# One group for both directions in the levels of the recurrent stage

## The chip, the cores and the metric

The kernel runs on one core of one Trainium2 chip. The metric is the time of one execution on the device, in microseconds (us). TensorE (PE) does matmuls into PSUM, VectorE (DVE) and ScalarE (ACT) read PSUM and write SBUF, GpSimd (POOL) does elementwise work in SBUF, and SyncE (SP) issues most transfers.

## The reference

Two layers of an encoder trunk with 512 tokens and a width of 1024. Layer 0 mixes the tokens with a bidirectional recurrence (RWKV-7, 8 heads of 64) beside a gating MLP, layer 1 with differential attention; each then has cross-attention into 256 memory tokens and a gated MLP with a convolution. The change concerns the recurrence alone. For each head and each direction a 64 x 64 state is carried from token to token:

```python
def rwkv7_step(state, inp):
    r, w, k, v, kk, a = inp
    sa = jnp.einsum('...vk,...k->...v', state, -kk)
    state = (state * w[..., None, :]
             + sa[..., :, None] * (kk * a)[..., None, :]
             + v[..., :, None] * k[..., None, :])
    y = jnp.einsum('...vk,...k->...v', state, r)
    return state, y

def rwkv7_bidirectional(z, mu_prev, mu_next, w0, w2, a0, a2, g2, k_k, k_a, r_k, out_gain):
    ...
    state0 = jnp.zeros((2, bsz, H, N, N), jnp.float32)
    _, ys = lax.scan(rwkv7_step, state0, xs)
    y = ys[:, 0] + jnp.flip(ys[:, 1], axis=0)
    y = rms_norm(jnp.transpose(y, (1, 0, 2, 3)), out_gain).astype(z.dtype)
    bonus = jnp.sum(rh[:, :, None] * kh * r_k, axis=(2, 4))
    out = (y + bonus[..., None] * vh).reshape(bsz, seq, RWKV_WIDTH)
    return out * g
```

## The kernel before

All is fp32. The large products of the rest of the kernel run as three fp32r products (`gemm_pe`, line 369), with the weights split by ScalarE and VectorE. Between them lies the recurrent stage, `pair_pe`, `pair_act`, `pair_dve` and `pair_pool`, once for each of NJ = 4 pairs of heads.

The recurrence isn't run token by token. The 512 tokens are cut in chunks of CH = 64. In a chunk the dependence of each token on the earlier ones is a triangular 64 x 64 matrix, and the kernel needs the inverse of (I - A). For a pair of heads there are 2 directions (d = 0 forward, 1 backward) x 8 units (head and token tile) x 2 halves of the partitions (x), 32 blocks of 64 x 64. A tile such as UU has the shape [128, 2, 8, 64]: one direction is 128 x 512, both are 128 x 1024.

The inverse is built by doubling. `gram_dve` (line 1170) makes AI, and the first U and T, which are right inside blocks of 2. Then LV = 5 levels double the block size. A level does:
- X: TensorE multiplies AI by U for each block (line 938), direction 0 into PSUM bank 0 and direction 1 into bank 2;
- mask: VectorE multiplies that by the level's 0/1 mask into XX (line 1231), one instruction for each direction, when `p_x` tells that the direction's 16 matmuls are done;
- U: TensorE multiplies T by XX (line 952) into the same bank, when `p_xm` tells that the direction's mask is done;
- T: TensorE multiplies the other way round (line 958) into banks 1 and 3, except at the last level;
- copies: ScalarE copies U (line 1071) and T (line 1075) of each direction back to SBUF, which releases the next level's X (`p_u0`, `p_u1`) and U (`p_t0`, `p_t1`) for that direction.

The order on TensorE is written out: X of direction 0, X of direction 1, `side_pe` (work of this or the next pair that fits in between), `chain_pe` (a step of the chunk-to-chunk chain of the previous pair), then U and T of direction 0, U and T of direction 1, `side_pe` and `chain_pe` again. In pair 0 there is no chain, in pair 3 there is no next pair to prepare, so there the gaps hold less. Side work and chain use banks 4 to 7. After the levels the product at line 972 multiplies U by AXT, waiting for each direction's U, and a tail of small products (lines 980 and 1010) and the next pair's Gram products (lines 832 and 844) follow. VectorE does in a level the two masks, then the additions of the chain (lines 877 and 881), and from level 2 on the next pair's decay scan, keys and scaling (`prep_scan_dve`, `prep_key_dve`, `prep_scale_dve`). ScalarE does in a level side copies, the copies of U and T, side copies. Each fp32 product shows as two MATMUL rows in the trace, so a group of 16 is x32 there.

Of the kernel before, what the change touches and what calls it, by code (L numbers as in the profile page):

```python
# [25 lines left out]
P = 128  # L26
# [64 lines left out]
def build(nc, a, out):  # L91
# [718 lines left out]

    def mask24(name):
        return rk(name).unsqueeze(1).unsqueeze(1).to_broadcast([P, 2, NT, CH])
# [113 lines left out]
    def pair_pe(T, j):  # L926
        e = T.e
        gram_pe(T, j)
        for lv in range(LV):
            for d in range(2):  # L930
                e.wait_ge(S(f"p_u{d}"), j * (LV + 1) + lv + 1)
                if lv == 0 and d == 0:
                    e.wait_ge(S("p_bfree"), 2 * j + 2)
                if lv == 0 and d == 1 and j > 0:
                    e.wait_ge(S("p_qfree"), j)
                for u in range(8):
                    for x in range(2):
                        mm = e.matmul(PS[xs(x), 2 * d, u * CH:u * CH + CH], AI[xs(x), d, u, :], UU[xs(x), d, u, :],  # L938
                                      start=True, stop=True)
                mm.then_inc(S("p_x"), 1)  # L940
            side_pe(T, j, 2 * lv)
            if j > 0 and 1 <= 2 * lv <= STEPS:
                chain_pe(e, j - 1, 2 * lv)
            for d in range(2):
                e.wait_ge(S("p_xm"), 2 * (j * LV + lv) + d + 1)
                if lv == 0:
                    e.wait_ge(S("p_tt"), 2 * j + d + 1)
                else:
                    e.wait_ge(S(f"p_t{d}"), j * (LV - 1) + lv)
                for u in range(8):  # L950
                    for x in range(2):
                        mm = e.matmul(PS[xs(x), 2 * d, u * CH:u * CH + CH], TT[xs(x), d, u, :], XX[xs(x), d, u, :],  # L952
                                      start=True, stop=True)
                mm.then_inc(S(f"p_un{d}"), 1)
                if lv < LV - 1:
                    for u in range(8):
                        for x in range(2):
                            mm = e.matmul(PS[xs(x), 2 * d + 1, u * CH:u * CH + CH], XX[xs(x), d, u, :], TT[xs(x), d, u, :],  # L958
                                          start=True, stop=True)
                    mm.then_inc(S(f"p_tn{d}"), 1)  # L960
# [6 lines left out]
        for d in range(2):  # L967
            e.wait_ge(S(f"p_u{d}"), (j + 1) * (LV + 1))
# [96 lines left out]
    def pair_act(A, j):  # L1065
        e = A.e
        for lv in range(LV):
            side_act(A, j, 2 * lv)
            for d in range(2):
                e.wait_ge(S(f"p_un{d}"), j * LV + lv + 1)  # L1070
                e.activation(UU[:, d, :, :], PS[:, 2 * d, :].rearrange("p (u k) -> p u k", k=CH), ACT.Copy)\
                    .then_inc(S(f"p_u{d}"), 1)
                if lv < LV - 1:
                    e.wait_ge(S(f"p_tn{d}"), j * (LV - 1) + lv + 1)
                    e.activation(TT[:, d, :, :], PS[:, 2 * d + 1, :].rearrange("p (u k) -> p u k", k=CH), ACT.Copy)\
                        .then_inc(S(f"p_t{d}"), 1)
            side_act(A, j, 2 * lv + 1)
# [92 lines left out]
    def gram_dve(V, j):  # L1170
# [10 lines left out]
        for d in range(2):  # L1181
            V.mine(e.tensor_tensor(AI[:, d, :, :], AI[:, d, :, :], mask8("ident2"), ALU.add))
            V.wait_mine()
            e.tensor_tensor(UU[:, d, :, :], UU[:, d, :, :], mask8("ident2"), ALU.add).then_inc(S(f"p_u{d}"), 1)
# [40 lines left out]
    def pair_dve(V, j):  # L1225
        e = V.e
        gram_dve(V, j)
        for lv in range(LV):
            for d in range(2):
                e.wait_ge(S("p_x"), 2 * (j * LV + lv) + d + 1)  # L1230
                e.tensor_tensor(XX[:, d, :, :], PS[:, 2 * d, :].rearrange("p (u k) -> p u k", k=CH),
                                mask8(f"X{'fb'[d]}{lv + 2}"), ALU.mult).then_inc(S("p_xm"), 1)
# [832 lines left out]
```

## Time and profile before

| what | value |
|---|---|
| median of 3 runs | 1934.67 us (1932.86 to 1935.8) |
| the profiled execution | 1930.15 us, span 1928.3 us |
| mean granted TensorE clock | 0.981 of full |
| busy: TensorE | 1807.2 us (94%) |
| busy: VectorE, ScalarE, GpSimd | 997.2, 778.8, 100.9 us |
| chain that ended last | TensorE 86%, VectorE 7%, ScalarE 3%, issue 2% |
| of it line 369 / 952 / 958 / 938 | 67% / 2% / 2% / 1% |
| recurrent stage | 177 to 421 us |

Busy time is the time in which an engine's rows cover the clock; the end of a matmul row is modelled. The chain is followed back from the last instruction to what released each step. A row of the timeline gives start, length, engine, line, operation, tiles, how many instructions it merges, and in brackets how long the engine was idle ahead of it and what ended that.

### The profile page before, as it was taken

The numbers are of one execution on the slowest core, as the hardware profiler recorded it, in microseconds if no ns is written. First come the engines' busy times: TensorE is split into PE (matmuls) and PEld (weight loads), VectorE is DVE, ScalarE is ACT, GpSimd is POOL, SyncE is SP. The second block draws the span as 40 slices with busy tenths as digits, with TensorE's granted clock in tenths as the row PEclk, the third lists the DMA queues.
The fourth block names the chain that finished last, engine by engine and source line by source line (L and its number), as shares of the span: only waits on it lengthen the run. The fifth ranks groups of instructions, "written<-read, shape, count | busy, mean of one in ns | idle before, by whom it ended". The sixth has DMA issues, their size and how long they took to land.

```text
span 1928.3 us, 32260 instructions
## 1 busy us (share of the span) xinstructions
PE 1807.2 (94%) x14281; PEld 1494.3 (77%) x14281; DVE 997.2 (52%) x1355; ACT 778.8 (40%) x1166; POOL 100.9 (5%) x79
## 2 busy tenths in 40 slices
PE   4998998889899999999998999999999999999999
PEld 4877887777777878888887887567777878888887
DVE  4477555547524355634553444795524346543662
ACT  3243443343554244422432333774545244422441
POOL 1001111100000000000000022000000000000000
PEclk9999999989999999999999999999999999999999
DMA  6310000033322223322322222002322122233222
GB/s 209 98 44 1 4 3 4 4 112 119 110 88 88 66 66 110 109 88 88 90 97 98 88 88 88 1 1 75 123 87 88 54 77 88 91 109 107 87 77 76
DMA packets 96453, 149.41 MB, mean 77 GB/s; under 512 B 3479, under 2 KB 50170, under 8 KB 96314
## 3 DMA queue, kind: packets, MB, share of 16 engines
q1 hardware_dynamic: 95018, 142.41, 22.5%
q0 software_dynamic: 1296, 4.95, 0.8%
q8 instruction: 112, 1.84, 0.4%
q14 instruction: 27, 0.22, 0.0%
HBM read 145.25 MB, written 2.10 MB: 76 GB/s over the span
## 4 chain that ended last, share of the span: by engine, by line
PE 86%; DVE 7%; ACT 3%; issue 2%; DMA 1%; POOL 0%; ACTq 0%; DVEq 0%; POOLq 0%; SPq 0%
PE PS L369 67%; PE PS L1452 3%; PE PS L952 2%; PE PS L958 2%; PE PS L1469 1%; PE PS L938 1%; PE PS L1338 1%; PE PS L1312 1%; PE PS L495 1%; DMA WRAW<-ab_w_in 1%; PE PS L980 1%; PE PS L972 1%; DVE LOS L444 1%; PE PS L1459 1%; DVE WLO L338 1%
## 5 line engine op out<-in xcount | busy, mean ns | idle before, releaser
L338 DVE TENSOR_TENSOR WLO<-WRAW,WHI 128x2048 fp32r<-128x2048 f32 (+1 forms) x132 | 296.5, 2250 | 445.2 <-ACT WHI L330 445.2
L330 ACT ACTIVATE WHI<-WRAW 128x2048 fp32r<-128x2048 f32 (+1 forms) x132 | 248.0, 1881 | 484.5 <-PE PS L369 451.2
L369 PE MATMUL PS<-HIS,WHI 128*128 128x512 f32 x856 | 333.8, 390 | 1.5 <-DVE SM L1699 1.5
L369 PE MATMUL PS<-HIS,WLO 128*128 128x512 f32 x856 | 333.0, 389 | 0.0
L369 PE MATMUL PS<-LOS,WHI 128*128 128x512 f32 x856 | 333.0, 389 | 0.0
L369 PE MATMUL PS<-WHI,HIS 128*128 128x512 f32 x608 | 238.9, 393 | 11.0 <-DVE LOS L444 4.0
L369 PE MATMUL PS<-WHI,LOS 128*128 128x512 f32 x608 | 238.0, 391 | 0.0
L369 PE MATMUL PS<-WLO,HIS 128*128 128x512 f32 x608 | 237.9, 391 | 0.0
L369 PEld LDWEIGHTS PS<-HIS,WHI 128*128 128x128 f32 x856 | 160.7, 188 | 35.2 <-DVE SM L1699 1.9
L369 PEld LDWEIGHTS PS<-HIS,WLO 128*128 128x128 f32 x856 | 160.7, 188 | 33.6
L369 PEld LDWEIGHTS PS<-LOS,WHI 128*128 128x128 f32 x856 | 160.7, 188 | 33.4 <-issue 0.2
L369 PEld LDWEIGHTS PS<-WHI,HIS 128*128 128x128 f32 x608 | 114.9, 189 | 37.6 <-DVE LOS L444 4.4
L369 PE MATMUL PS<-WHI,GHI 128*128 128x512 f32 x352 | 136.9, 389 | 0.0
L369 PE MATMUL PS<-WHI,GLO 128*128 128x512 f32 x352 | 136.9, 389 | 0.0
L369 PE MATMUL PS<-WLO,GHI 128*128 128x512 f32 x352 | 136.9, 389 | 0.0
L369 PEld LDWEIGHTS PS<-WLO,HIS 128*128 128x128 f32 x608 | 115.0, 189 | 24.2
L369 PEld LDWEIGHTS PS<-WHI,LOS 128*128 128x128 f32 x608 | 114.9, 189 | 23.6
L502 DVE TENSOR_TENSOR X<-X,PS 128x512 f32<-128x512 f32 x64 | 42.9, 684 | 70.6 <-PE PS L369 70.6
L369 PEld LDWEIGHTS PS<-WLO,GHI 128*128 128x128 f32 x352 | 66.1, 188 | 13.8
L369 PEld LDWEIGHTS PS<-WHI,GLO 128*128 128x128 f32 x352 | 66.1, 188 | 13.7
L369 PEld LDWEIGHTS PS<-WHI,GHI 128*128 128x128 f32 x352 | 66.1, 188 | 13.7
L1415 ACT ACTIVATE GHI<-SG 128x512 fp32r<-128x512 f32 x44 | 27.8, 633 | 108.9 <-DVE SG L1435 108.9
(281 smaller groups left out, 2519.0 us busy)
## 6 DMA issues: line engine op xcount, KB each, us to landing
WRAW<-ffn_w_up SPq DMA_DIRECT2D x88, 512.0 KB, 4.7
WRAW<-ffn_w_down SPq DMA_DIRECT2D x20, 1024.0 KB, 5.0
WRAW<-cross_wkv SPq DMA_DIRECT2D x16, 1024.0 KB, 5.0
WRAW<-diff_w_in SPq DMA_DIRECT2D x12, 1024.0 KB, 5.1
WRAW<-ab_w_in SPq DMA_DIRECT2D x10, 1024.0 KB, 5.3
WRAW<-cross_wq SPq DMA_DIRECT2D x8, 1024.0 KB, 5.0
WRAW<-cross_wo SPq DMA_DIRECT2D x8, 1024.0 KB, 5.1
X<-x SPq DMA_DIRECT2D x8, 512.0 KB, 9.1
```

The source lines that it names most:

```text
L330: A.e.activation(part(WHI[i % 3], i), part(WRAW[i % 2], i), ACT.Copy).then_inc(S("w_hi"), 1)
L338: V.e.tensor_tensor(part(WLO[i % 3], i), part(WRAW[i % 2], i), part(WHI[i % 3], i).bitcast(F32), ALU.subtract).then_inc(S("w_lo"), 1)
L369: mm = e.matmul(o, l, r, start=(si == 0 and kk == 0 and q == 0), stop=(si == len(steps) - 1 and kk == nk - 1 and q == 2))
L444: e.scalar_tensor_tensor(lo(k)[:, 0:nt * P], PS[:, b0 + k % 4, 0:nt * P], gain(k), hi(k)[:, 0:nt * P].bitcast(F32), ALU.mult, ALU.subtract ...
L495: mm = e.transpose(PS[:, b0 + k % 4, t * P:t * P + P], xn[:, t, k * P:k * P + P], ident)
L502: V.e.tensor_tensor(o, o, PS[:, bank_base(name, gi) + b, :], ALU.add).then_inc(sem(name, "ev"), 1)
L938: mm = e.matmul(PS[xs(x), 2 * d, u * CH:u * CH + CH], AI[xs(x), d, u, :], UU[xs(x), d, u, :], start=True, stop=True)
L952: mm = e.matmul(PS[xs(x), 2 * d, u * CH:u * CH + CH], TT[xs(x), d, u, :], XX[xs(x), d, u, :], start=True, stop=True)
L958: mm = e.matmul(PS[xs(x), 2 * d + 1, u * CH:u * CH + CH], XX[xs(x), d, u, :], TT[xs(x), d, u, :], start=True, stop=True)
L972: mm = e.matmul(PS[xs(x), 2 * d + u // 4, (u % 4) * P:(u % 4) * P + P], UU[xs(x), d, u, :], AXT[xs(x), d, u, :], start=True, stop=True)
L1415: A.e.activation(GHI[2 * gi + b - 2][:, :], SG[b - 2][:, :], ACT.Copy).then_inc(sem(name, "hi"), 1)
L1452: e.matmul(PS[:, b + c, :], QF[:, h, c, t * P:t * P + P], KF[:, h, :], start=True, stop=True).then_inc(S("dl"), 1)
```

## The change

The two directions are no longer two groups. At each level TensorE does the X of both directions (banks 0 and 1) and signals once; VectorE multiplies both by their masks in one instruction of 1024 columns (`mask2x8` addresses the forward and backward mask with one stride); TensorE then does U of both directions, signals, T of both directions (banks 2 and 3), signals; ScalarE copies U of both in one instruction and T of both in another. The first U of a pair (`gram_dve`) is signalled once, after both directions (`p_u0`). The product at line 972 waits for the one copy of U. The matmuls are the same in number and shape.

```diff
--- before.py
+++ after.py
@@ -807,6 +807,12 @@
 
     def mask8(name):
         return rk(name).unsqueeze(1).to_broadcast([P, 8, CH])
+
+    def mask2x8(lv):
+
+        o = RK[f"Xf{lv}"][0]
+        by = RK["Xb2"][0] - RK["Xf2"][0]
+        return RC[:, o:o + 2 * by].rearrange("p (d k) -> p d k", d=2)[:, :, 0:CH].unsqueeze(2).to_broadcast([P, 2, 8, CH])
 
     def mask24(name):
         return rk(name).unsqueeze(1).unsqueeze(1).to_broadcast([P, 2, NT, CH])
@@ -927,37 +933,40 @@
         e = T.e
         gram_pe(T, j)
         for lv in range(LV):
+            if lv == 0:
+                e.wait_ge(S("p_u0"), j + 1)
+                e.wait_ge(S("p_bfree"), 2 * j + 2)
+                if j > 0:
+                    e.wait_ge(S("p_qfree"), j)
+            else:
+                e.wait_ge(S("p_un"), j * LV + lv)
             for d in range(2):
-                e.wait_ge(S(f"p_u{d}"), j * (LV + 1) + lv + 1)
-                if lv == 0 and d == 0:
-                    e.wait_ge(S("p_bfree"), 2 * j + 2)
-                if lv == 0 and d == 1 and j > 0:
-                    e.wait_ge(S("p_qfree"), j)
                 for u in range(8):
                     for x in range(2):
-                        mm = e.matmul(PS[xs(x), 2 * d, u * CH:u * CH + CH], AI[xs(x), d, u, :], UU[xs(x), d, u, :],
+                        mm = e.matmul(PS[xs(x), d, u * CH:u * CH + CH], AI[xs(x), d, u, :], UU[xs(x), d, u, :],
                                       start=True, stop=True)
-                mm.then_inc(S("p_x"), 1)
+            mm.then_inc(S("p_x"), 1)
             side_pe(T, j, 2 * lv)
             if j > 0 and 1 <= 2 * lv <= STEPS:
                 chain_pe(e, j - 1, 2 * lv)
+            e.wait_ge(S("p_xm"), j * LV + lv + 1)
+            if lv == 0:
+                e.wait_ge(S("p_tt"), 2 * j + 2)
+            else:
+                e.wait_ge(S("p_tn"), j * (LV - 1) + lv)
             for d in range(2):
-                e.wait_ge(S("p_xm"), 2 * (j * LV + lv) + d + 1)
-                if lv == 0:
-                    e.wait_ge(S("p_tt"), 2 * j + d + 1)
-                else:
-                    e.wait_ge(S(f"p_t{d}"), j * (LV - 1) + lv)
                 for u in range(8):
                     for x in range(2):
-                        mm = e.matmul(PS[xs(x), 2 * d, u * CH:u * CH + CH], TT[xs(x), d, u, :], XX[xs(x), d, u, :],
+                        mm = e.matmul(PS[xs(x), d, u * CH:u * CH + CH], TT[xs(x), d, u, :], XX[xs(x), d, u, :],
                                       start=True, stop=True)
-                mm.then_inc(S(f"p_un{d}"), 1)
-                if lv < LV - 1:
+            mm.then_inc(S("p_u"), 1)
+            if lv < LV - 1:
+                for d in range(2):
                     for u in range(8):
                         for x in range(2):
-                            mm = e.matmul(PS[xs(x), 2 * d + 1, u * CH:u * CH + CH], XX[xs(x), d, u, :], TT[xs(x), d, u, :],
+                            mm = e.matmul(PS[xs(x), 2 + d, u * CH:u * CH + CH], XX[xs(x), d, u, :], TT[xs(x), d, u, :],
                                           start=True, stop=True)
-                    mm.then_inc(S(f"p_tn{d}"), 1)
+                mm.then_inc(S("p_t"), 1)
             side_pe(T, j, 2 * lv + 1)
             if j > 0 and 2 * lv + 1 <= STEPS:
                 if lv == 0:
@@ -965,7 +974,7 @@
                 chain_pe(e, j - 1, 2 * lv + 1)
 
         for d in range(2):
-            e.wait_ge(S(f"p_u{d}"), (j + 1) * (LV + 1))
+            e.wait_ge(S("p_un"), (j + 1) * LV)
             e.wait_ge(S("p_ax"), 2 * j + d + 1)
             for u in range(8):
                 for x in range(2):
@@ -1066,14 +1075,13 @@
         e = A.e
         for lv in range(LV):
             side_act(A, j, 2 * lv)
-            for d in range(2):
-                e.wait_ge(S(f"p_un{d}"), j * LV + lv + 1)
-                e.activation(UU[:, d, :, :], PS[:, 2 * d, :].rearrange("p (u k) -> p u k", k=CH), ACT.Copy)\
-                    .then_inc(S(f"p_u{d}"), 1)
-                if lv < LV - 1:
-                    e.wait_ge(S(f"p_tn{d}"), j * (LV - 1) + lv + 1)
-                    e.activation(TT[:, d, :, :], PS[:, 2 * d + 1, :].rearrange("p (u k) -> p u k", k=CH), ACT.Copy)\
-                        .then_inc(S(f"p_t{d}"), 1)
+            e.wait_ge(S("p_u"), j * LV + lv + 1)
+            e.activation(UU[:, :, :, :], PS[:, 0:2, :].rearrange("p d (u k) -> p d u k", k=CH), ACT.Copy)\
+                .then_inc(S("p_un"), 1)
+            if lv < LV - 1:
+                e.wait_ge(S("p_t"), j * (LV - 1) + lv + 1)
+                e.activation(TT[:, :, :, :], PS[:, 2:4, :].rearrange("p d (u k) -> p d u k", k=CH), ACT.Copy)\
+                    .then_inc(S("p_tn"), 1)
             side_act(A, j, 2 * lv + 1)
         for d in range(2):
             e.wait_ge(S("p_wu"), 2 * j + d + 1)
@@ -1181,7 +1189,8 @@
         for d in range(2):
             V.mine(e.tensor_tensor(AI[:, d, :, :], AI[:, d, :, :], mask8("ident2"), ALU.add))
             V.wait_mine()
-            e.tensor_tensor(UU[:, d, :, :], UU[:, d, :, :], mask8("ident2"), ALU.add).then_inc(S(f"p_u{d}"), 1)
+            i = e.tensor_tensor(UU[:, d, :, :], UU[:, d, :, :], mask8("ident2"), ALU.add)
+        i.then_inc(S("p_u0"), 1)
         for d in range(2):
             e.tensor_tensor(TT[:, d, :, :], AI[:, d, :, :], mask8(M_T1[d]), ALU.mult).then_inc(S("p_tt"), 1)
 
@@ -1226,10 +1235,9 @@
         e = V.e
         gram_dve(V, j)
         for lv in range(LV):
-            for d in range(2):
-                e.wait_ge(S("p_x"), 2 * (j * LV + lv) + d + 1)
-                e.tensor_tensor(XX[:, d, :, :], PS[:, 2 * d, :].rearrange("p (u k) -> p u k", k=CH),
-                                mask8(f"X{'fb'[d]}{lv + 2}"), ALU.mult).then_inc(S("p_xm"), 1)
+            e.wait_ge(S("p_x"), j * LV + lv + 1)
+            e.tensor_tensor(XX[:, :, :, :], PS[:, 0:2, :].rearrange("p d (u k) -> p d u k", k=CH), mask2x8(lv + 2),
+                            ALU.mult).then_inc(S("p_xm"), 1)
             if lv == 0:
                 gram_k_dve(V, j)
             for s in (2 * lv, 2 * lv + 1):
```

On TensorE, in level 1 of pair 0, the row that begins an X group (lines 938 and 946) waits for U, the row that begins a U group (952 and 960) for T and for the mask; L817 and L823 are the side work. Before:

```order
L938 MATMUL PS<-UU,AI 64x64 [waits p_u0]
L938 MATMUL PS<-UU,AI 64x64 x15
L938 MATMUL PS<-UU,AI 64x64 [waits p_u1]
L938 MATMUL PS<-UU,AI 64x64 x15
L817 MATMUL PS<-ZS_86,WL_71 128x512 [waits p_bonfree]
L817 MATMUL PS<-ZS_86,WL_71 128x512
L952 MATMUL PS<-XX,TT 64x64 [waits p_t0,p_xm]
L952 MATMUL PS<-XX,TT 64x64 x15
L958 MATMUL PS<-TT,XX 64x64 x16
L952 MATMUL PS<-XX,TT 64x64 [waits p_t1,p_xm]
L952 MATMUL PS<-XX,TT 64x64 x15
L958 MATMUL PS<-TT,XX 64x64 x16
```

And with the change, in the same place on TensorE:

```order
L946 MATMUL PS<-UU,AI 64x64 [waits p_un]
L946 MATMUL PS<-UU,AI 64x64 x31
L823 MATMUL PS<-ZS_86,WL_71 128x512 [waits p_bonfree]
L823 MATMUL PS<-ZS_86,WL_71 128x512
L960 MATMUL PS<-XX,TT 64x64 [waits p_tn,p_xm]
L960 MATMUL PS<-XX,TT 64x64 x31
L967 MATMUL PS<-TT,XX 64x64 x32
```

The T product of direction 0 moved from ahead of the U product of direction 1 to behind it, and a level has two rows that wait for another engine's work on X or U where it had four.

On ScalarE, from the copies of level 3 of pair 0 to those of WU after level 4 (TMP is the exponentials of the next pair, AXT side work), before:

```order
L1071 ACTIVATE UU<-PS 128x512 [waits p_un0]
L1075 ACTIVATE TT<-PS 128x512 [waits p_tn0]
L1071 ACTIVATE UU<-PS 128x512 [waits p_un1]
L1075 ACTIVATE TT<-PS 128x512 [waits p_tn1]
L1033 ACT_TABLE_LOAD
L1033 ACTIVATE TMP_109<-TMP_111 128x1024 [waits p_c]
L1035 ACTIVATE TMP_111<-TMP_111 128x1024 [waits p_e]
L1062 ACTIVATE AXT<-PS 128x8x64 [waits p_x0] x2
L1071 ACTIVATE UU<-PS 128x512 [waits p_un0]
L1071 ACTIVATE UU<-PS 128x512 [waits p_un1]
L1080 ACTIVATE WU_97<-PS 128x1024 [waits p_wu]
```

The same stretch of ScalarE with the change:

```order
L1079 ACTIVATE UU<-PS 128x1024 [waits p_u]
L1083 ACTIVATE TT<-PS 128x1024 [waits p_t]
L1042 ACT_TABLE_LOAD
L1042 ACTIVATE TMP_109<-TMP_111 128x1024 [waits p_c]
L1044 ACTIVATE TMP_111<-TMP_111 128x1024 [waits p_e]
L1071 ACTIVATE AXT<-PS 128x8x64 [waits p_x0] x2
L1079 ACTIVATE UU<-PS 128x1024 [waits p_u]
L1088 ACTIVATE WU_97<-PS 128x1024 [waits p_wu]
```

Nothing changed places here; four copies became two, and the two after level 4 became one, which waits for the U product of both directions.

## Rows read from the trace of the kernel before

**Rows 1.** Waits of TensorE, 177 to 421 us: waited for, total us, times, longest.
```profile
PE PS L952 <- DVE XX L1231: 7.9, 8, 2.0
PE PS L1010 <- issue: 6.5, 4, 1.9
...
PE PS L938 <- DVE UU L1184: 4.8, 8, 1.3
PE PS L980 <- issue: 4.8, 4, 1.3
```

**Rows 2.** Windows: stretch, its us, busy us of each engine, clock, DMA.
```profile
178.00:181.00 3.00, 3.00 (x76) 3.00 (x72) 1.82 (x3) 0.00 (x0) 0.00 (x0) 0.50 0.02 5
238.00:241.00 3.00, 2.13 (x76) 1.89 (x68) 2.97 (x6) 0.00 (x0) 0.00 (x0) 1.00 0.00 0
177.00:421.00 244.00, 214.65 (x6934) 196.82 (x6931) 126.96 (x211) 92.72 (x147) 30.23 (x21) 0.99 0.03 7
```

**Rows 3.** Timeline of level 2, pair 0: start, us, engine, line, work.
```profile
201.50 2.08 PE L938 MATMUL PS<-UU,AI 64*64 64x64 f32 x64
...
203.63 0.69 DVE L1231 TENSOR_TENSOR XX<-PS,RC 128x512 f32<-128x512 f32 x1 [0.24 <-PE PS L938]
...
204.15 1.15 PE L952 MATMUL PS<-XX,TT 64*64 64x64 f32 x32
...
209.06 2.08 PE L938 MATMUL PS<-UU,AI 64*64 64x64 f32 x64
```

**Rows 4.** Single lines: length in ns, least, median, most.
```profile
L1071 ACT ACTIVATE UU<-PS x40: 597/597/601, 189.0 to 404.7; 128x512 f32<-128x512 f32 x40
...
L1141 DVE TENSOR_TENSOR KAP<-TMP,TMP x4: 1210/1210/1215, 158.8 to 348.7; 128x1024 f32<-128x1024 f32 x4
...
L1080 ACT ACTIVATE WU<-PS x8: 1024/1026/1030, 223.7 to 408.2; 128x1024 f32<-128x1024 f32 x8
```

**Rows 5.** Timeline of level 0, pair 0, TensorE.
```profile
185.90 1.15 PE L938 MATMUL PS<-UU,AI 64*64 64x64 f32 x32 [0.18 <-DVE UU L1184]
...
187.70 1.15 PE L952 MATMUL PS<-XX,TT 64*64 64x64 f32 x32 [0.66 <-DVE XX L1231]
```

**Rows 6.** Timeline: U of level 3 pair 0, level 2 pair 1, level 1 pair 3.
```profile
212.09 1.15 PE L952 MATMUL PS<-XX,TT 64*64 64x64 f32 x32
...
259.81 2.03 PE L938 MATMUL PS<-UU,AI 64*64 64x64 f32 x64
...
261.89 0.69 DVE L1231 TENSOR_TENSOR XX<-PS,RC 128x512 f32<-128x512 f32 x1 [0.24 <-PE PS L938]
...
262.93 1.10 PE L952 MATMUL PS<-XX,TT 64*64 64x64 f32 x32
...
376.37 1.80 PE L938 MATMUL PS<-UU,AI 64*64 64x64 f32 x56
...
378.70 1.10 PE L952 MATMUL PS<-XX,TT 64*64 64x64 f32 x32
```

**Rows 7.** Timeline of level 3, pair 1 (pair 2 reads alike).
```profile
273.23 1.26 DVE L1231 TENSOR_TENSOR XX<-PS,RC 128x512 f32<-128x512 f32 x2
273.95 1.15 PE L952 MATMUL PS<-XX,TT 64*64 64x64 f32 x32 [1.98 <-DVE XX L1231]
```

**Rows 8.** Timeline of level 4: pair 0, pair 1 and pair 3.
```profile
219.55 1.95 PEld L952 LDWEIGHTS PS<-XX,TT 64*64 64x64 f32 x64
...
221.66 3.59 PE L972 MATMUL PS<-AXT,UU 64*64 64x128 f32 x61
...
282.51 2.08 PE L952 MATMUL PS<-XX,TT 64*64 64x64 f32 x64 [0.64 <-DVE XX L1231]
...
284.42 3.55 PE L972 MATMUL PS<-AXT,UU 64*64 64x128 f32 x61
...
402.60 2.03 PE L952 MATMUL PS<-XX,TT 64*64 64x64 f32 x64
...
404.47 3.55 PE L972 MATMUL PS<-AXT,UU 64*64 64x128 f32 x62
```

## The prediction

> **What bounds the kernel now.** I read the waits of TensorE first, then the stage as a whole, then single levels in order of time. The change touches only the recurrent stage, from 177 to 421 us of a span of 1928.3 us. There TensorE has work for 214.65 of 244 us, VectorE for 126.96, ScalarE for 92.72, and the granted clock is 0.99, the 2.4 GHz level [rows 2]. The reader should see that TensorE's idle time in this stage is short and has few causes: 7.9 us until a mask of VectorE (8 times), 4.8 us until the first U of a pair is ready (8 times), and some 14 us in which nothing held it but its own instructions, 6.5 us of it at line 1010 and 4.8 us at line 980 [rows 1]. No row there shows TensorE waiting for a copy of U or T, except for a few tenths after the last level.
>
> Now a single level, level 2 of pair 0 [rows 3]. TensorE starts the X group of both directions at 201.50. VectorE starts the mask of the second direction at 203.63, 2.13 us after the group began. But the mask of the first direction has been ready for long, and TensorE goes from X through its side work straight into the first U group at 204.15, 2.65 us after X began, and into the next X at 209.06, with no wait on those rows. So in such a level **TensorE's issue is the bound**, and the split in two directions is what hides the mask: the first direction's mask runs under the second direction's matmuls. The same split hides the copies.
>
> **The change, part by part.** No matmul is removed. A level loses one mask instruction and two copies (one at level 4), and gets wide ones.
>
> *Wide instructions.* A mask of 512 columns releases U 0.72 us after its start (273.23 to 273.95) [rows 7]. For 1024 columns the nearest row is VectorE's product at line 1141, 1.21 us; with the same 0.03 us of hand-over that gives 1.24 us. The copy of 512 columns takes 0.60 us and the 1024-column copy of line 1080 takes 1.03, so 0.43 more [rows 4]. These have the same source and type, so I take them as they are; the upper bound is twice a narrow one (0.69 and 0.60, so 1.38 and 1.20, 0.17 more each) [rows 3, 4], and no row supports less than 1.21 and 1.03, which are the lower ends too.
>
> *The mask before U.* The wide mask can start only when the X of both directions is done: 2.13 us after X began in pair 0 [rows 3], 2.08 us in the later pairs, where no idle or switch stands ahead (259.81 to 261.89) [rows 6]. So U can't start before X + 3.37 us in pair 0 and X + 3.32 us in the others. What covers this is TensorE's side and chain work between X and U. Where it is shorter, the difference is new idle time.
> - Level 0: there is no side work, and the first X also waits now for the U of both directions, so it starts at 185.90 instead of 184.57. 185.90 + 2.13 + 1.24 = 189.27 against 187.70 [rows 5]: 1.57 us, alike in all four pairs, **6.28 us**.
> - Level 1: in pair 0 the distance from X to U is 3.07 us (it lacks a chain step), so 0.30. In pairs 1 and 2 it is over 3.5, so nothing. In pair 3 there is no next pair to prepare, and it is 378.70 - 376.37 = 2.33 [rows 6], so 0.99. **1.29 us**.
> - Level 2: pair 0 has 2.65 us [rows 3], so 0.72. The others have 262.93 - 259.81 = 3.12 [rows 6], so 0.20 each. **1.32 us**.
> - Level 3: pair 0 has 212.09 - 209.06 = 3.03 [rows 3, 6], so 0.34. In pairs 1 and 2 VectorE is late with its scans and the mask starts at 273.23 in any case [rows 7]; U follows 1.24 instead of 0.72 later, 0.52 each. Pair 3 has 3.5, nothing. **1.38 us**.
> - Level 4: side work (line 922, as many rows as X) makes the distance from X to U four groups too, 3.73, in pairs 0 and 3, nothing there. In pairs 1 and 2 VectorE's keys are late as at level 3 and U waited already (0.64 us on its row) [rows 8]: 0.52 each, counted in the next item.
>
> *The copy after U.* At levels 0 to 3 the copy of U has the whole T group and the side work of TensorE to hide in: it is ready 2.13 + 1.03 + 0.12 = 3.28 us after U began, the next X starts 3.73 us after it at the earliest (four groups of 0.93, from 2.08 for 64 rows less 1.15 for 32 [rows 5, 8]). The copy of T has the next X and its mask. Both cost nothing; if that cover were gone, 0.43 us plus half a group each. After level 4 there is no T, and line 972 waits for U. Today the first direction's copy is enough to start it. Now U of both must be done (0.93 us more, a group of 64 rows takes 2.08 and one of 32 takes 1.15) [rows 5, 8] and be copied (0.43 more): 1.36 us in pair 3 (404.47 to 405.83). With the late mask, 0.52 + 1.36 = 1.88 in pairs 1 and 2 each. In pair 0 ScalarE is late with its exponentials, which hides a part: U is done at 219.55 + 2.08 = 221.63, its copy releases line 972 at 222.78 against 221.66 [rows 8], 1.12. **6.24 us**.
>
> *VectorE's and ScalarE's other work.* Behind each mask on VectorE stand the K masks (level 0), the chain's additions and the next pair's preparation; they start up to 0.6 us later against X, but later X groups are later too, and TensorE waits for them only where it is counted above. On ScalarE line 1041, 1027 and 1048 follow the copies with over 0.3 us to spare. SP and POOL get no instruction moved; the first load of the next weights waits for the end of this stage and moves with it.
>
> Sum: 6.28 + 1.29 + 1.32 + 1.38 + 6.24 = **16.5 us slower**. The profiled execution, 1930.15 us, would become 1946.7. The median of the runs shown is 4.5 us above that execution, so for the median I say 1934.67 + 16.5 = 1951.2 us.
>
> A rule that speaks for the change: two masks in a row cost 1.26 us on VectorE [rows 7], because the second overlaps the first, against 1.21 for a wide one [rows 4], so 0.05 us is saved per level. The Trainium skill (VectorE: DVE Perf Modes, "The TRN2 errata") says that each instruction pays a fixed latency once, so that one large tile is cheaper than two small ones; by its formula for fp32, an estimate, a merge saves 0.157 us, 3.1 us over 20 levels. The trace shows a third of it, on an engine that is idle for half of the stage.
>
> **The rivals.**
> 1. *Faster: the ring of three engines is the bound, not TensorE's issue.* If X, mask, U, copy and the next X were one chain at every level, then merging saves the fixed costs: 0.05 us for each of 20 masks and 2 x 0.60 - 1.03 = 0.17 for each of 36 copies, 7.1 us, giving 1927.6. It decides from the point where the *second* direction's mask or copy ends after TensorE's own work. Against it: between 201.50 and 209.06 TensorE has none of these waits [rows 3], and 7.9 us in all stand on masks [rows 1].
> 2. *TensorE's code comes too late in the tail of each pair, and takes up the new waits.* Lines 980 and 1010 hold four gaps each, in the middle of groups that wait for no semaphore [rows 1]. If they are code that is not loaded yet, a wait just ahead of them lets it arrive. The new wait before line 972 could then hide the first gap of each pair: 4.8 us back, 1946.4. If all 11.3 us went, 1939.9. Against it: the stretch before line 972 is slower than the tail, so its code is there in time already, and the matmuls are as many as before. The Trainium skill (Runtime: NRT & Kernel Launch, "Instruction fetch mechanics") says that code fetch is hidden, as an engine dispatches slower than the code comes in. By that there would be no such gaps, nothing would be given back, and the sum would stand; the 6.5 and 4.8 us speak against the page.
> 3. *The clock falls in the new gaps.* At 1.2 GHz (granted 0.50) 76 rows of line 844 and its neighbours filled 3.00 us, at the full clock 76 rows filled 2.13 [rows 2]. If each pair ran some 9 us around level 4 at the low clock, that is 4 x 3 x 0.87 = 10.4 us more, 1961.6. Against it: from 238 to 241 TensorE was idle for almost a third and kept 1.00 [rows 2], and the longest new gap is under 3 us.
> 4. *No difference*, within 4 us: everything that adds is hidden by the late code and the chain of VectorE. It needs rival 2 in full (5.2 us are left) and 1.3 us more, 1938.6 or less.
>
> **How the numbers follow.** The forecast has 0.73, rival 1 has 0.05, rival 2 has 0.11, rival 3 has 0.06 and rival 4 has 0.05. The bounds of the wide instructions are 0.17 for the mask in the 15 levels that count (2.6 us) and 4 x 0.17 for copies (0.7); a session's median moves by 2 us, as the runs and the profiled execution show. That gives 1946.5 to 1956 for the forecast alone; rival 2's first case lies at its lower edge, and the range is 1945 to 1957. A measurement of this kernel can tell about 0.2% (3.9 us) from no change. Slower 0.90, within it 0.06, faster 0.04 (rival 1, less what its saving is too small to show).
>
> **What would show it.** Waits of the U group for the mask rise from 7.9 to some 15 us, with 1.3 us at level 0 of each pair and 2.5 at level 3 of pairs 1 and 2. The waits of the first X of a pair rise from 4.8 to some 9 us. The group of line 972 gets a wait for ScalarE's U of 1.1 us in each pair, 4.6 us in all, where there was none. The mask takes 1.21 us and starts 2.1 us after X; U and T copies take 1.03. TensorE's busy time in the stage stays at 215 us and the stage grows by 16.5. I am wrong if the gaps at lines 980 and 1010 shrink by several us (rival 2), if matmul rows get longer (rival 3), or if the wide mask takes well over 1.4 us.

## The result, and the profile after

The changed kernel takes 1949.43 us (median of 4 runs, 1946.98 to 1952.37); the kernel before, beside it, 1933.76 us (4 runs, 1930.38 to 1935.8). The ratio is 1.0088, 95% interval 1.0069 to 1.0107: slower by about 17.0 us (the medians differ by 15.7). The prediction was 16.5 us slower, 1951.2 us in a range of 1945 to 1957. The profiled execution takes 1946.98 us, against 1930.15 for that of before.

The page of the changed kernel, its span and the busy time of the engines:

```profile
span 1945.2 us, 32181 instructions
...
PE 1807.0 (93%) x14281; PEld 1494.5 (77%) x14281; DVE 994.8 (51%) x1335; ACT 772.2 (40%) x1130; POOL 99.9 (5%) x79
```

The span grew by 16.9 us. The waits of TensorE in the recurrent stage of the changed kernel, 177 to 441 us (line waited for, total us, times, longest), answer to [rows 1]; lines 946, 960, 989 and 1019 are the 938, 952, 980 and 1010 of before:

```profile
PE PS L960 <- DVE XX L1239: 14.8, 12, 2.5
PE PS L946 <- DVE UU L1192: 10.0, 4, 2.6
PE PS L1019 <- issue: 6.5, 4, 1.9
PE PS L989 <- issue: 5.3, 4, 1.6
PE PS L981 <- ACT UU L1079: 4.5, 4, 1.1
```

Three rows changed, and they are the three that the working named: the mask 7.9 to 14.8 us, the first X of a pair 4.8 to 10.0, and a new wait of 4.5 us for the copy of U. The two rows of gaps in which TensorE waits for no other engine stayed: 6.5 and 6.5, 4.8 and 5.3. The three are 14.8 + 10.0 + 4.5 = 29.3 us now and were 7.9 + 4.8 = 12.7: 16.6 us more, against the 16.9 us by which the span grew.

The stage as a whole, from the first Gram row of pair 0 to the first row of the chain behind the last tail, before and changed (us, busy us of PE, PEld, DVE, ACT and POOL, clock, DMA):

```profile
176.72:418.18 241.46, 212.52 (x6880) 195.15 (x6881) 125.35 (x205) 92.72 (x147) 30.23 (x21) 0.99 0.02 4
```

```profile
175.40:436.00 260.60, 214.59 (x6880) 196.54 (x6881) 122.95 (x185) 86.63 (x111) 29.31 (x21) 0.98 0.02 4
```

Between these two marks the stage is 19.1 us longer. TensorE does the same 6880 matmul rows in 214.59 us, 2.1 more than before; its idle time grew from 28.9 to 46.0 us, by 17.1. VectorE and ScalarE have 2.4 and 6.1 us less to do. So nearly all of the added time is idle time of TensorE.

Level 2 of pair 0, the stretch of [rows 3], in the timeline of the changed kernel:

```profile
201.89 2.08 PE L946 MATMUL PS<-UU,AI 64*64 64x64 f32 x64
...
204.01 1.22 DVE L1239 TENSOR_TENSOR XX<-PS,RC 128x1024 f32<-128x1024 f32 x1 [7.12 <-PE PS L946]
...
205.29 2.08 PE L960 MATMUL PS<-XX,TT 64*64 64x64 f32 x64 [0.68 <-DVE XX L1239]
...
207.42 1.02 ACT L1079 ACTIVATE UU<-PS 128x1024 f32<-128x1024 f32 x1 [1.68 <-PE PS L960]
```

The wide mask starts 2.12 us after X and lasts 1.22; U starts 3.40 us after X, where it was 2.65. Before the change the first mask ran under the second direction's matmuls; now nothing of X is left to run under it. The copy of U ends at 208.44 and the next X comes at 210.20, so that copy is hidden, as forecast.

Level 0 of pair 0 [rows 5] in the changed kernel, with both new waits one behind the other:

```profile
184.34 2.08 PE L946 MATMUL PS<-UU,AI 64*64 64x64 f32 x64 [2.60 <-DVE UU L1192]
...
186.47 1.23 DVE L1239 TENSOR_TENSOR XX<-PS,RC 128x1024 f32<-128x1024 f32 x1 [0.98 <-PE PS L946]
...
187.75 2.08 PE L960 MATMUL PS<-XX,TT 64*64 64x64 f32 x64 [1.33 <-DVE XX L1239]
```

The wide instructions themselves (ns: least, median, most), against [rows 4]:

```profile
L1239 DVE TENSOR_TENSOR XX<-PS,RC x20: 1197/1224/1225, 186.5 to 417.2; 128x1024 f32<-128x1024 f32 x20
```

```profile
L1079 ACT ACTIVATE UU<-PS x20: 1023/1023/1027, 190.0 to 420.9; 128x1024 f32<-128x1024 f32 x20
```

They took 1.224 and 1.023 us; 1.21 and 1.03 were borrowed from other lines.

Level 3 of pair 1 [rows 7] and level 4 of pair 1 [rows 8] in the changed kernel:

```profile
279.21 2.08 PE L960 MATMUL PS<-XX,TT 64*64 64x64 f32 x64 [2.51 <-DVE XX L1239]
```

```profile
288.30 2.08 PE L960 MATMUL PS<-XX,TT 64*64 64x64 f32 x64 [1.18 <-DVE XX L1239]
291.50 3.60 PE L981 MATMUL PS<-AXT,UU 64*64 64x128 f32 x61 [1.12 <-ACT UU L1079]
```

Waits of 1.98 and 0.64 us became 2.51 and 1.18, 0.53 and 0.54 more. The product after the levels starts 3.20 us after U instead of 1.91.

### The profile page after: what moved, and what is told of

The parts are those of the page before. It is cut to its first block, busy times and chain, and to the rows that moved or that the text cites. A ratio compares the mean times of both kernels' runs of the same rounds, so it can differ in the third digit from the quotient of the medians.

```text
span 1945.2 us, 32181 instructions
## 1 busy us (share of the span) xinstructions
PE 1807.0 (93%) x14281; PEld 1494.5 (77%) x14281; DVE 994.8 (51%) x1335; ACT 772.2 (40%) x1130; POOL 99.9 (5%) x79
## 3 DMA queue, kind: packets, MB, share of 16 engines
q0 software_dynamic: 1296, 4.95, 0.8%
## 4 chain that ended last, share of the span: by engine, by line
PE 84%; DVE 8%; ACT 4%; issue 2%; DMA 2%; POOL 0%; ACTq 0%; POOLq 0%; SPq 0%; DVEq 0%
PE PS L369 64%; PE PS L1460 3%; PE PS L960 2%; PE PS L946 2%; PE PS L967 2%; PE PS L1477 1%; PE PS L1346 1%; DVE WLO L338 1%; PE PS L495 1%; PE PS L1320 1%; DVE XX L1239 1%; DMA WRAW<-ab_w_in 1%; PE PS L989 1%; PE PS L981 1%; DMA WRAW<-cross_wq 1%
```

## The experiments

The sizes below are distances between starts of groups on TensorE, read from the timelines: X to U, U to the product after the levels, Gram to the first X of a pair. Ratios are to the kernel before, measured beside each kernel on the same chip. Each kernel has one profile (the changed kernel two), and its execution is not always near the median of the timed runs.

### One part undone at a time

**x_mask**: the changed kernel with one mask per direction, each signalled and waited for alone (VectorE's side is shown; U of a direction waits for its own mask).

```diff
+            for d in range(2):
+                e.wait_ge(S("p_x"), 2 * (j * LV + lv) + d + 1)
+                e.tensor_tensor(XX[:, d, :, :], PS[:, d, :]..., mask8(f"X{'fb'[d]}{lv + 2}"), ALU.mult)...
```

> The changed kernel with the X group and the mask by direction again: TensorE signals X of each direction, VectorE masks 512 columns at a time, U of a direction waits for its own mask. Copies and the first U stay wide. Theory A (TensorE goes without a gap as long as something covers the mask; what costs is that nothing of U can start before X of both directions is done and masked): U follows X after 1.9 us instead of 3.4 at level 0, and at the other levels as soon as the side work ends, which gives back 4 x 1.5 at level 0, and 1.4, 1.5, 1.4 and 1.1 us at levels 1 to 4, 11.5 us: about 1938. Theory B (the cost is in the order U, U, T, T, the banks, or the wide copies): under half of it comes back, over 1943.

Measured: 1939.2 us, ratio 1.0042 (1.003 to 1.0055). TensorE's waits in the stage:

```profile
PE PS L946 <- DVE UU L1192: 9.9, 4, 2.6
...
PE PS L960 <- DVE XX L1240: 5.3, 4, 2.0
```

The wait for the mask is gone except at levels 3 and 4 of pairs 1 and 2, and the distance from X to U at levels 1 to 4 is that of before to 0.01 us (3.07, 2.66, 3.04, 3.73 in pair 0). The first X still waits 9.9 us. 8.9 us came back (1.0088 less 1.0042), where 11.5 were expected. At level 0 the expected 1.9 us came in pairs 0 and 1 (1.94 each); in pairs 2 and 3 X to U was 2.70 and 3.41, and the granted clock had fallen to 0.50 there (at 309.6 and 374.4 us) and once at level 3 of pair 1 (at 275.4). So the wide mask carries about half of the loss. The parts are not quite separate: 1.94 is also 1.19 below the 3.13 of the kernel before, since both first U are ready when X begins.

**x_copy**: after level 4 alone, U of each direction is signalled and copied by itself, with direction 1 in bank 2 there (levels 0 to 3 stay wide).

> The changed kernel with U of the last level copied by direction, each copy with its own signal, and with direction 1 in bank 2 at that level. Theory A: the first product after the levels starts 1.9 us after U instead of 3.2 (1.1 in pair 0), 5.0 us in all: about 1944.5. Theory B (the first half of that product would wait for something else, such as AXT): no difference, 1949.

Measured: 1949.4 us, ratio 1.0089 (1.0074 to 1.0103), no gain. Yet the edit did what it was for: U to the product after the levels is 2.47, 1.91, 1.92 and 1.87 us in the four pairs, where the changed kernel has 3.16 to 3.20: 4.5 us. The gain went somewhere else, and TensorE's timeline of level 0, pair 0, shows where:

```profile
184.60 2.55 PE L946 MATMUL PS<-UU,AI 64*64 64x64 f32 x64 [2.63 <-DVE UU L1201]
...
188.47 2.83 PE L960 MATMUL PS<-XX,TT 64*64 64x64 f32 x48 [1.32 <-DVE XX L1248]
```

The same waits as in the changed kernel, but the matmuls are slower: 64 rows of X take 2.55 instead of 2.08. X to U is 3.87, 4.91, 4.56 and 4.57 us in the four pairs, where the changed kernel has 3.41 each time. With the next U to X, the slow rows at level 0 cost 7.5 us. This is the clock; it has a part of its own below. The profile explains the loss inside the stage (261.98 us long, the changed kernel 260.60). This execution, 1943.52 us, is also the fastest of the six: outside the stage it took 1679.7 us, the changed kernel 1684.6. Why the median lies 5.9 us higher stays open.

**x_first**: the first U of a pair is signalled by direction again.

> The changed kernel with the first U of a pair signalled by direction. X of direction 0 starts 1.3 us earlier in each pair, but the wide mask waits for X of direction 1, which ends 0.9 to 1.0 us earlier. Theory A: 4 x 0.95 = 3.8 us back, about 1945.6. Theory B (VectorE's own order holds the mask back, which stands behind the T masks): under 1 us, 1949.

Measured: 1944.7 us, ratio 1.0067 (1.0053 to 1.008). The wait of the first X falls from 10.0 to 4.9 us; X to U of level 0 grows from 3.41 to 3.71, since the second direction's X now starts with its own late U.

**x_all3**: these three undone together. What stays of the change: one wide copy of U at levels 0 to 3 and one of T, the other banks, and the order U, U, T, T on TensorE.

> The three together: masks, first U and last copy by direction. What stays of the change is its banks, its order U, U, T, T, and one wide copy of U (levels 0 to 3) and of T. Theory A says that those are hidden and cost nothing: the time of the kernel before, 1933.8 within 2 us. Theory B: 1938 or more.

Measured: 1930.05 us, ratio 0.9995 (0.9986 to 1.0005), 12 runs. TensorE's waits:

```profile
PE PS L961 <- DVE XX L1249: 7.9, 8, 2.0
...
PE PS L947 <- DVE UU L1202: 4.5, 4, 1.4
```

The rows are those of before (7.9 and 4.8). The whole loss is in the three merged hand-overs; the copies at levels 0 to 3, the banks and the order of the matmuls together cost at most 1.0 us and give at most 2.7. Rival 1, a ring of engines as the bound, would have the wide copies gain 0.17 us each, 5.4 us for 32: the interval excludes it.

### What is left where VectorE is late

**early_before** and **early_after**: the next pair's preparation on VectorE goes between the two chain steps of its level, in the kernel before and in the changed one.

```diff
             for s in (2 * lv, 2 * lv + 1):
                 if j > 0 and 1 <= s <= STEPS:
                     chain_dve(e, j - 1, s)
-            if j + 1 < NJ and lv >= 2:
-                (prep_scan_dve, prep_key_dve, prep_scale_dve)[lv - 2](V, j + 1)
+                if j + 1 < NJ and lv >= 2 and s == 2 * lv:
+                    (prep_scan_dve, prep_key_dve, prep_scale_dve)[lv - 2](V, j + 1)
```

> The kernel before with one line moved on VectorE: in levels 2 to 4 the next pair's scan, keys and scaling stand between the two additions of the chain instead of behind both. Nothing else differs. Theory A (at levels 3 and 4 of pairs 1 and 2 the mask is late only since that work is queued behind an addition that waits for TensorE, while VectorE idles): the distance from X to U falls from 5.65 to 3.5 us at level 3 and from 4.55 to 3.7 at level 4, 5.9 us in all: about 1928. Theory C (VectorE has too much work there in any order, or GpSimd slows it): under 2 us, 1932 or more.

> The same move in the changed kernel. Theory A: from 6.18 to 3.5 us at level 3 and from 5.08 to 3.7 at level 4 of pairs 1 and 2, 8.0 us in all: about 1941.5, so that the part of the change that was paid there (2.1 us) is not paid any more and the distance to the kernel before with the same move is 13.5 to 14.5 us. Theory C: under 2 us.

Measured: early_before 1923.98 us, ratio 0.9964 (0.995 to 0.9978): faster than both kernels. X to U at level 3 of pairs 1 and 2 falls from 5.65 to 3.50 us, at level 4 from 4.55 to 3.73, 2 x (2.15 + 0.82) = 5.9 us in all. The timeline of early_before:

```profile
263.76 0.69 DVE L1102 TENSOR_SCALAR TMP<-TMP 128x1024 f32<-128x1024 f32 x1
...
268.71 2.03 PE L938 MATMUL PS<-UU,AI 64*64 64x64 f32 x64
...
269.85 0.69 DVE L1231 TENSOR_TENSOR XX<-PS,RC 128x512 f32<-128x512 f32 x1 [0.64 <-PE PS L938]
```

And of the kernel before, the same instruction and its neighbour on GpSimd:

```profile
268.03 2.36 POOL L1152 TENSOR_TENSOR BET<-KK,TMP 128x1024 f32<-128x1024 f32 x1 [6.14 <-PE PS L914]
...
268.72 2.22 DVE L1102 TENSOR_SCALAR TMP<-TMP 128x1024 f32<-128x1024 f32 x1
```

The instruction took 2.22 us, now 0.69, and it no longer stands ahead of the mask: it now comes 4.7 us before GpSimd's product, in a stretch in which VectorE was idle. In the kernel before it ended at 270.94, 0.55 us after GpSimd's product (270.39). The Trainium skill (SBUF — State Buffer, "Who interferes with whom") says that this kind of VectorE instruction can take the port pair shared with GpSimd, and that the one of the two that comes second blocks fully until the first is done. The trace agrees in time: 1.67 of the 2.22 us lie under GpSimd's product, and all four of these instructions take 0.68 to 0.69 us in early_before. How much of the gain comes from this and how much from the new place was not tested apart.

early_after: 1944.35 us, ratio 1.0066 (1.0053 to 1.0078): about 4.3 us back (1.0088 less 1.0066) where 8.0 were expected, and about 20 us above early_before where 13.5 to 14.5 were expected. The same distances came down (3.50 and 3.73), but X to U at level 0 of pairs 2 and 3 is 4.57 and 4.25 instead of 3.41, with the clock down at 311.6 and 376.5 us; with a slower U to X in pair 3 that is 3.6 us.

**cover_after**: the changed kernel with the VTK half of line 980's products, which needs no U, put ahead of the product that waits for the copy.

> The changed kernel with the products of GKR and VTK, which need no U, moved from behind the first product after the levels to ahead of it. They fill TensorE's wait for the wide copy. Theory A (the wide copy of U costs only because nothing covers it): 4 x 1.0 = 4.0 us back, about 1945.4. Theory B (the copy delays the tail in another way, or the code of the tail comes later then): no difference.

Measured: 1950.87 us, ratio 1.01 (1.0085 to 1.0114), no gain. The cover is there (TensorE goes from U straight into it):

```profile
225.21 2.03 PE L960 MATMUL PS<-XX,TT 64*64 64x64 f32 x64
227.20 1.16 PE L980 MATMUL PS<-GKR,VTK 64*64 64x64 f32 x64
228.37 3.60 PE L1001 MATMUL PS<-AXT,UU 64*64 64x128 f32 x62
```

The stretch from that product to the next Gram is 1.8, 1.5 and 1.4 us shorter in the first three pairs. But level 0 is slow in all four pairs: X to U 3.90, 4.03, 4.95 and 4.51, with the next U to X 8.8 us lost in all.

### The clock at level 0

Two experiments that removed a stall of TensorE without touching level 0, x_copy and cover_after, had lost their gain at level 0, and early_after a part of it. To see whether the changed kernel does this by itself, it ran unedited once more.

> The changed kernel once more, beside the next three. Theory K (in the merged kernels TensorE idles twice around the first X of a pair, and in some executions the clock falls to the 1.2 GHz level there, as in the traces of x_copy and cover_after, at a different number of pairs each time): 1.0088 of the kernel before, with one or more pairs whose distance from the first X to U is over 3.5 us. Theory A alone: the same time, and 3.41 us in every pair.

Measured: 1951.88 us, ratio 1.0091 (1.0076 to 1.0106). Windows of level 0, pair 0:

```profile
183.00:186.00 3.00, 1.23 (x42) 1.23 (x44) 2.88 (x5) 0.00 (x0) 0.00 (x0) 1.00 0.02 5
186.00:189.00 3.00, 1.67 (x36) 1.49 (x34) 1.56 (x2) 0.00 (x0) 0.00 (x0) 0.51 0.00 0
189.00:192.00 3.00, 3.00 (x62) 3.00 (x61) 2.05 (x4) 0.00 (x0) 0.00 (x0) 0.50 0.00 0
```

After a stretch in which TensorE was idle for 1.77 of 3 us the granted clock is 0.50, the 1.2 GHz level, and from 189 to 192 it is busy throughout and does 62 rows. The fall itself stands inside the X group, at 186.08 us:

```profile
184.77 2.62 PE L946 MATMUL PS<-UU,AI 64*64 64x64 f32 x64 [2.64 <-DVE UU L1192]
188.72 1.55 PE L960 MATMUL PS<-XX,TT 64*64 64x64 f32 x24 [1.33 <-DVE XX L1239]
```

```profile
184.77:186.08 1.31, 1.31 (x44) 1.31 (x46) 1.15 (x2) 0.00 (x0) 0.00 (x0) 1.00 0.00 0
186.08:187.39 1.31, 1.31 (x28) 1.12 (x22) 0.00 (x0) 0.00 (x0) 0.00 (x0) 0.50 0.00 0
```

The first 1.31 us of X have 1.00 and the rest 0.50. So the fall follows one idle time, the 2.64 us until the first U; the 1.33 us until the mask come after it. X to U is 3.95 and the next U to X 7.68 instead of 5.79: 2.4 us lost. The first profile of the same kernel had 1.00 there and one short fall, in the Gram at 305.3 us (0.72 from 304 to 307):

```profile
304.00:307.00 3.00, 2.09 (x77) 2.09 (x80) 0.14 (x1) 1.09 (x2) 2.32 (x3) 0.72 0.02 5
307.00:310.00 3.00, 3.00 (x87) 3.00 (x83) 2.58 (x5) 0.00 (x0) 0.00 (x0) 0.71 0.03 5
```

This one follows the 1.91 us gap at line 1019, in which TensorE waited for no other engine, and no new wait. So the places of the falls differ between executions of one kernel. In the profiled executions of before, early_before, x_first and x_all3, in which the first X comes by direction, no fall stands at level 0; in after_again, x_mask, x_copy, early_after and cover_after, where the merged wait is kept, there are two to four; in the first profile of the changed kernel there is none. A fall at level 3 is in x_first (at 278.9 us, behind a 2.51 us wait for the mask) and in x_all3 (at 336.5, behind the 1.98 us wait that the kernel before has too). In every profile a fall inside the levels stands behind one idle time of 2.0 to 2.6 us, in its last 0.8 us or at most 1.5 us after its end; other waits of the same length have none.

The test: fill TensorE's idle time at level 0. **fill_** kernels add two 128x512 products ahead of the wait for the first U and one between X and U, with results that nobody reads. The wait `p_qfree` moves ahead of them. The matmuls of the computation stay.

```diff
             if lv == 0:
+                if j > 0:
+                    e.wait_ge(S("p_qfree"), j)
+                for q in range(2):
+                    e.matmul(PS[:, 3, :], rk("bones"), KK[:, j, :], start=True, stop=True)
                 e.wait_ge(S("p_u0"), j + 1)
...
             mm.then_inc(S("p_x"), 1)
+            if lv == 0:
+                e.matmul(PS[:, 3, :], rk("bones"), KK[:, j, :], start=True, stop=True)
```

> The changed kernel with three products of 128x512 that nobody reads, into bank 3, at level 0 of each pair: two in TensorE's wait for the first U, one in its wait for the mask. They fill idle time only. Theory K: the granted clock stays at 1.00 through every level 0, the first X to U takes 3.4 us in all four pairs, and 2 to 4 us come back (1.0067 to 1.0078 of the kernel before). Theory A alone: no gain, or 0.5 us lost where the products do not fit in.

> x_copy with the same three products at level 0. Theory K: the 5.0 us that the copy by direction gives back, which the timed runs of x_copy did not show, show now: kernel before + 11.5 us (1.0060). If the gain of the copy was lost elsewhere than in the clock: no better than x_copy (1.0089).

> cover_after with the same three products at level 0. Theory K: the 4 us that the moved products of GKR and VTK give back show now: kernel before + 12.5 us (1.0065), against 1.0100 without the filling. Otherwise: 1.009 or more.

The last two columns are the length of the stage in the profile, in us, between the same two marks as above (241.46 in the kernel before):

| kernel | without filling | with filling | stage without | stage with |
|---|---|---|---|---|
| changed | 1.0091 (1.0076 to 1.0106) | 1.0084 (1.0069 to 1.0098) | 263.53 (first profile 260.60) | 260.44 |
| x_copy | 1.0089 (1.0074 to 1.0103) | 1.0050 (1.0036 to 1.0064) | 261.98 | 257.20 |
| cover_after | 1.0100 (1.0085 to 1.0114) | 1.0050 (1.0037 to 1.0063) | 263.40 | 257.25 |
| early_after | 1.0066 (1.0053 to 1.0078) | 1.0046 (1.0032 to 1.006) | 254.84 | 249.64 |

The timeline of fill_after, level 0 of pair 0, shows the first two products (four records, 1.98 us) in the place of the idle time, and X's wait down from 2.60 to 0.47 us:

```profile
183.87 1.98 PE L940 MATMUL PS<-KK,RC 128*128 128x512 f32 x4
186.32 2.08 PE L948 MATMUL PS<-UU,AI 64*64 64x64 f32 x64 [0.47 <-DVE UU L1196]
```

In all four filled kernels X to U at level 0 is 3.41 us in every pair (3.40 to 3.41). Adding work that nobody needs made x_copy 0.39% faster and cover_after 0.50%. These are 7.5 and 9.7 us; the stage in the profiles is 4.8 and 6.1 us shorter, and the clock accounts for about that: the slow rows at level 0 (7.5 and 8.8 us) are gone, and the slow rows behind the mask's wait at level 3 cost 2.9 us in both with the filling, none and 1.2 without it. For the changed kernel by itself, and for early_after, the intervals overlap: of the time nothing is shown. The changed kernel was expected at 1.0067 to 1.0078 and missed that with 1.0084, though level 0 came as expected. Which of the three products matter was not tried. Windows of fill_after, level 0 of pair 0 and level 3 of pair 1:

```profile
183.00:186.00 3.00, 2.85 (x40) 1.37 (x32) 2.93 (x6) 0.00 (x0) 0.00 (x0) 1.00 0.03 5
280.00:283.00 3.00, 2.48 (x46) 2.48 (x48) 0.86 (x3) 0.00 (x0) 0.00 (x0) 0.57 0.00 0
```

Level 0 keeps 1.00, but the clock now falls behind the 2.5 us wait of level 3, in pairs 1 and 2 (U to X 5.51 and 5.56 instead of 4.01). If that is so, removing that wait too should let the filling show. **fill_early** is early_after with the filling.

> early_after with the three unread products at level 0. In fill_after the clock no longer fell at level 0, but at the end of level 3 of pairs 1 and 2, behind the longest wait that was left (2.5 us for the mask), and only 1.5 us came back. The move on VectorE takes that wait away. Theory K: no fall of the clock inside the levels of any pair, and the sum of the traces is met: kernel before + 16.5 - 8.0 = + 8.5 us (1.0044), against 1.0066 for early_after. Otherwise: the clock falls at another place again, and the ratio stays at 1.006 or more.

Measured: 1939.9 us, ratio 1.0046 (1.0032 to 1.006). The levels have no fall left; one stands at 236.5 us, between two pairs. Against fill_after it gives back 7.3 us (1.0084 less 1.0046). In the profiles the stage is 10.8 us shorter: the two shortened levels are 2 x (2.68 + 1.34) = 8.0, and the two falls at level 3, 1.5 us each, are gone. The copy's wait stays, 1.1 us a pair, and the mask's is down to 3.2 us (it was 14.8; the unread product stands in 4.2 us of it, the move on VectorE takes 7.4):

```profile
PE PS L985 <- ACT UU L1083: 4.5, 4, 1.1
...
PE PS L964 <- DVE XX L1243: 3.2, 8, 0.9
```

Rival 3 is thus true of the changed kernel in small: it pays 1.2 to 2.4 us at some of the levels 0 and 3, in some executions, not 10.4 us around level 4. The Trainium skill (TensorE: Matmul & The Clock Gate, "A second HAM failure mode: psum-queue depth-cycling") says of another kernel that frequent short idle times between groups of matmuls make the clock swing between its levels and that the throughput then pays for it. The traces agree on the price, 1.2 to 2.4 us for a fall; here one idle time of 2.0 to 2.6 us stands before each fall at the levels, and no run shows that many short ones do it. What decides whether a given execution falls stays open: the waits are the same in both profiles of the changed kernel.

## Why the prediction was right

Each term, against what the two profiles show (us):

| term | forecast | measured |
|---|---|---|
| level 0 | 6.28 | 7.65 (from Gram to first X 6.54, from X to U 1.11) |
| level 1 | 1.29 | 1.37 |
| level 2 | 1.32 | 1.46 |
| level 3 | 1.38 | 1.45 |
| level 4 and the copy | 6.24 | 6.03 (mask 1.07, copy 4.96) |
| sum | 16.5 | 17.96 |

From the Gram of pair 0 to the end of the tail behind the last levels the stage is 19.1 us longer (175.40 to 436.00 against 176.72 to 418.18): the 17.96 and 1.2 in the tails, the other distances and rounding. The stage began 1.3 us earlier and what follows it took 0.9 less, so the span grew by 16.9. I did not trace these two; they are of the size by which runs differ. So that the forecast met the span to half a microsecond is in part luck: the stage was to grow by 16.5 us and grew by 19.1, and 2.2 us outside it came off again.

- *Levels 1 to 3* came out to 0.14 us each. The step that carried them, "X + 3.37 us in pair 0 and X + 3.32 us in the others" set against the distance that was there, measured 3.41 and 3.36.
- *Level 0* was sized too small. "1.57 us, alike in all four pairs" has two halves: the mask gave 0.28 instead of 0.24, and the first X came 1.09, 1.52, 1.77 and 2.16 us later after the Gram, not 1.33 each. In these stretches stand also the gaps of the Gram's own instructions and, in the third pair, the clock fall at 305.3; x_first gives back 1.24, 1.78 and 1.51 of it there.
- *Level 4*: 1.36 and 1.12 for the copy measured 1.28 and 1.11, the late mask 0.53 and 0.54 for 0.52.
- *Nothing for the copies of U at levels 0 to 3 and of T*: x_all3 confirms it at 0.9995.
- *The wide instructions*: "the same source and type" does not hold for the row at line 1141, which reads SBUF where the mask reads PSUM; the size was right all the same, 1.224 us for 1.21. The saving on VectorE was read off the one kind of place where the second mask overlaps the first (1.26 us for two). Where each mask stands alone (0.69 us), a merge saves 2 x 0.69 less 1.22, 0.16 us, which is the prediction's estimate of 0.157; over the 20 levels VectorE's busy time fell by 2.4 us. It bought nothing, as forecast.
- *The range*: its lower bound of 1946.5 does not follow from the terms given, of which only the 2 us of a session's median go downwards; the upper one does (2.6 + 0.7 + 2 above 1951.2).
- *Rival 2*, late code that takes up the new waits, fell: the gaps that wait for no other engine, the Gram's included, were 4.8 + 6.5 + 2.4 + 1.3 = 15.0 us and are 5.3 + 6.5 + 2.1 + 1.2 = 15.1, although a 1.1 us wait now stands ahead of each tail. That they wait for code is not refuted, and the traces have a sign of it: each of these gaps, 12 before and 10 now, ends 1.2 to 1.5 us after a transfer of 16 KB on the instruction queue has landed. Only the give-back did not come. *Rival 4* needed it and fell too.
- *Rival 3* was argued against with "from 238 to 241 TensorE was idle for almost a third and kept 1.00" and "the longest new gap is under 3 us". That argument was too weak: one idle time of 2.0 to 2.6 us was enough in some executions, and matmul rows got longer in after_again, which the prediction had named as a sign of this rival. It did not come at level 4. It stayed small beside the main sum, but it swallowed the whole gain of two experiments.

The parts undone agree with this roughly: x_mask takes 8.9 us off (1.0088 less 1.0042), x_first 4.1, and the copy's 4.5 to 5.0 show only where the idle time is filled: fill_copy stands 6.6 us below fill_after (1.0084 less 1.0050), its stage 3.2. That these come near the whole loss is no check of each part, since the clock took a share of every one of these times.

## What to carry to other kernels

Before merging two half-width instructions into one, ask which engine bounds the stretch. Where it is the engine that feeds them, the two halves are a pipeline: one wide mask saved VectorE some 0.1 us and made TensorE wait 0.2 to 1.0 us more, because it starts half a group later and lasts almost twice as long. Where the waiting engine has other work that covers the hand-over, as for T and U at levels 0 to 3, merging cost and gave nothing that these runs can tell. Look first for work that stands needlessly ahead of a late hand-over: moving it was worth 0.36% here.

## What I had not expected of the hardware

- TensorE's clock fell to its 1.2 GHz level behind a single idle time of 2.0 to 2.6 us, in one execution of a kernel and not in another. Filling the 2.6 us with two unneeded products of about 1.0 us each, and the next 1.3 us with a third, kept it at 1.00 there.
- A stall removed at one place can be paid back at another through the clock: in their profiles x_copy and cover_after were shorter where they were edited and slower at every level 0.
- A VectorE instruction of 0.69 us took 2.22 beside one of GpSimd that had begun 0.69 us earlier.
